# The copy of the turned queries or keys ahead of the exponential, in the last step of each attention unit

## The chip, the cores and the metric

The kernel runs on one NeuronCore of one Trainium2 chip. The metric is the device time of one execution in microseconds (us). Five engines work side by side, each through its own queue in order: TensorE (PE; its weight loads are shown apart as PEld), ScalarE (ACT), VectorE (DVE), GpSimd (POOL) and SyncE (SP), which issues most transfers. They meet through semaphores.

## What is computed

The reference runs two transformer blocks one after the other on 1024 tokens of width 1024. The change lies in the attention of the second block:

```python
def _attend_dense(q, k, v):
    s = jnp.einsum('bqhd,bkhd->bhqk', q, k, preferred_element_type=jnp.float32) * (QK_DIM ** -0.5)
    pr = jax.nn.softmax(s, axis=-1).astype(v.dtype)
    return jnp.einsum('bhqk,bkhd->bqhd', pr, v)

def _attend_latent(q, k_lat, v_lat, k_ctx, v_ctx):
    k_all = jnp.concatenate([k_lat, k_ctx], axis=1)
    v_all = jnp.concatenate([v_lat, v_ctx], axis=1)
    ...
```

There are 8 heads with queries and keys of 96 numbers and values of 64, 1024 queries in 8 blocks of 128, and 1280 keys (1024 of the tokens, 256 of the context). Ahead of it come the first block (windowed attention and a squared-ReLU network) and the second block's projections and Fourier mixer; behind it the merge of the two branches, a router and 16 experts.

## The kernel before, in words

**Precision.** Every operand of a matrix product is held as two parts: ACT copies a value and rounds it (the high part, "hi"), DVE subtracts that copy from the value (the low part, "lo"), and a product is three matmuls, hi by hi, hi by lo and lo by hi (`mm3`, lines 98 to 100). So whatever TensorE turns or multiplies passes through ACT and then DVE before TensorE can use it again.

**Rows and units.** A row `m` is one head and one block of 128 queries: head `m // 8`, block `m % 8`, 64 rows in all. Its logits are 128 by 1280. They stand in PSUM in one of two places, chosen by `m % 2` (`s_of`, line 2304), so the logits of row m+2 can be written only when the exponential of row m has been read out. A unit `u` is two rows, and there are 32 of them, four to a head (below they are called the units g = 0, 1, 2 and 3 of a head, g being `u % 4`). A unit has five steps t = 0 to 4, and the running number of a step is n = 5u + t. `STEPS` (line 2358) starts two units early, at n = -10.

**A step.** All three engines walk the same list of steps, each with a program of its own (`attn_pe` line 2432, `attn_act` line 2517, `attn_dve` line 2595). In step t of unit u, in this order:

- TensorE turns four 128 by 128 blocks of the exponentials of rows 2u and 2u+1 (line 2471) into one of two PSUM banks; multiplies turned blocks of earlier steps by the values (line 2482: one group of four in t = 0, 1 and 4, two in t = 3, none in t = 2); writes a piece of the logits of row 2u+4 or 2u+5 (lines 98 to 100); and in some steps turns a piece of queries or keys of a later head (line 2442) into the next of the two banks.
- ACT makes the high part of the turned exponentials (line 2572, tile MP_hi); runs an exponential over 128 by 1280 (line 2538, tile PB), that of row 2u+3 in t = 0 and that of row 2u+4 in t = 4; makes, where there is one, the high part of the turned queries or keys (line 2530, tiles qT_hi and kT_hi).
- DVE makes the low part of the turned exponentials (line 2665); in t = 2 the maximum of row 2u+4 and of the first 256 columns of row 2u+5 (lines 2613 and 2618), in t = 4 that of the other 1024 columns (line 2618) and the smaller of the two negated ones (line 2624); then the low part of the turned queries or keys (lines 2606 and 2608).

**Where queries and keys are turned** (`extra`, line 2320): queries of head h+2 in the last step (t = 4) of units 2 and 3 of head h, keys of head h+1 in the last step of units 0 and 1, and the last 256 keys in t = 1 of unit 0. So every last step has one, for as long as there is a later head: u = -2 to 25, 28 steps. In units 2 of heads 2, 4 and 6 ACT also spreads the inverse sums out in t = 0 and 1 (line 2581, tile `wide`, behind the exponential) and TensorE turns them in t = 1 and 2 (line 2509).

**The waits around it.** ACT's copy of turned queries or keys waits for TensorE's turning of them (line 2521). TensorE's logits wait in t = 0 for the exponential of row 2u+2, which is that of the last step of the unit before, and in t = 2 for that of row 2u+3 (line 2489). The two banks for turned blocks alternate: a turning waits until DVE has finished with the turning before the last (`t_free`, line 2413). Thus the turning in t = 1 waits for the low part of the queries or keys, and that in t = 2 for the low part of the turned exponentials of t = 0, or, where t = 1 turned something besides, for that of t = 1. The first logits of a new head, in t = 0 of unit 2, wait for the low part of the keys turned one step before (line 2492).

**The order is written twice.** `at_s` is a plan: a loop over the steps (lines 2365 to 2406) lists what each engine will finish, in order, and gives each entry its semaphore value; the programs assert that they come in that order. The change is therefore made in the plan and in `attn_act`.

Of the kernel before, what the change touches and what calls it, by code (L numbers as in the profile page):

```python
# [102 lines left out]
def _program(nc, A, out, ctx):  # L103
# [2194 lines left out]
    at_s = Stage(sem, "attn", pool=False)  # L2298
# [5 lines left out]
    def s_of(m, c0=0, c1=TA):  # L2304
        return S[:, TA * (m % 2) + c0:TA * (m % 2) + c1]

    def s_chunk(n):

        u, t = divmod(n, 5)
        m = 2 * u + 4  # L2310
        if not 0 <= m < 2 * N_U:
            return []
        return [[(m, 0, 512)], [(m, 512, 1024)], [(m, 1024, 1280), (m + 1, 0, 256)], [(m + 1, 256, 768)],
                [(m + 1, 768, 1280)]][t]

    def times_v_in(n):

        return [x for x in {0: (n - 2,), 1: (n - 2,), 2: (), 3: (n - 3, n - 2), 4: (n - 2,)}[n % 5] if 0 <= x < 5 * N_U]

    def extra(n):  # L2320


        u, t = divmod(n, 5)
        h, g = divmod(u, 4)
        x = {(2, 4): ("turn_q", h + 2, 0), (3, 4): ("turn_q", h + 2, 1), (0, 1): ("turn_k", h + 1, 2),
             (0, 4): ("turn_k", h + 1, 0), (1, 4): ("turn_k", h + 1, 1)}.get((g, t))
        if x and x[1] < 8:
            return x
        if 0 < t < 3 and (g == 2 and h in (2, 4, 6) or u == N_U - 1):
            return "row", 3 if u == N_U - 1 else h // 2 - 1, t - 1  # L2330
        return None

    def exp_at(n):

        u, t = divmod(n, 5)
        m = {0: 2 * u + 3, 4: 2 * u + 4}.get(t, -1)
        return m if 0 <= m < 2 * N_U else None

    def pair_of(n):

        u, t = divmod(n, 5)
        h, g = divmod(u, 4)
        return 3 if u >= N_U - 2 else h // 2 - 1 if h in (2, 4, 6) else None

    def is_invert(n):
        u, t = divmod(n, 5)
        return t == 4 and (u % 4 == 1 and u // 4 in (2, 4, 6) or u == N_U - 2)

    def is_wide(n):
        u, t = divmod(n, 5)  # L2350
        return t < 2 and (u % 4 == 2 and u // 4 in (2, 4, 6) or u == N_U - 1)

    def split_at(n):

        u, t = divmod(n, 5)
        return u - 28 if t == 4 and 28 <= u < 31 else None
# [8 lines left out]
    for n in STEPS:  # L2365
        u, t = divmod(n, 5)
        x = extra(n)
        if t == 2 and 0 < u <= N_U:
            at_s.act.plan(("low", u - 1))
            at_s.dve.plan(("out", u - 1))  # L2370
        if 0 <= n < 5 * N_U:
            at_s.pe.plan(("turn", n))
            at_s.act.plan(("turn", n))
            at_s.dve.plan(("turn", n))
            t_last.append(("turn", n))
        at_s.pe.plan(*[("times_v", x) for x in times_v_in(n)])
        if s_chunk(n) and t in (2, 4):
            at_s.pe.plan(("logits", 2 * u + 4 + t // 4))
            at_s.dve.plan(*(("max", 2 * u + 4), ("part", 2 * u + 5, 0)) if t == 2 else
                          (("part", 2 * u + 5, 1), ("max", 2 * u + 5)))  # L2380
        if exp_at(n) is not None:
            at_s.act.plan(("exp", exp_at(n)))
        if is_wide(n):
            at_s.act.plan(("wide", pair_of(n), t))
        if x:
            at_s.pe.plan(x)
            if x[0] != "row":
                at_s.act.plan(x)
                at_s.dve.plan(x)
            elif x[1] < 3:  # L2390
                at_s.dve.plan(x)
            if x[0:2] != ("row", 3):
                t_last.append(x)
        if is_invert(n):
            at_s.dve.plan(("inverse", pair_of(n)))
        if split_at(n) is not None:
            at_s.act.plan(("split", split_at(n)))
        if split_at(n - 2) is not None:
            at_s.dve.plan(("split", split_at(n - 2)))
        if n == 5 * N_U - 1:  # L2400
            at_s.dve.plan(("row", 3, 0))
            at_s.act.plan(("split", 3, 0))
        if n == 5 * N_U + 3:
            at_s.dve.plan(("split", 3, 0), ("row", 3, 1))
            at_s.act.plan(("split", 3, 1))
            at_s.dve.plan(("split", 3, 1))
# [3 lines left out]
    def t_bank(*x):  # L2410
        return B_MT[t_seq[x] % 2]
# [10 lines left out]
    def o_col(c):  # L2422
        return Q[:, :, 192 * c:192 * c + 128]

    def heads_of(who):
        return (Q, 8, qT) if who == "turn_q" else (K_, 10, kT2)
# [90 lines left out]
    def attn_act(act):  # L2517
        def turn_heads(who, h, i):
            D, nb, dst = heads_of(who)
            w = min(512, nb * P - 512 * i)  # L2520
            act.wait_ge(*at_s.pe(who, h, i))
            if h > 1:
                act.wait_ge(*at_s.pe("logits", 8 * (h - 2) + 7))
            elif (who, h) == ("turn_k", 1):
                act.wait_ge(*hd.pe("v", 9))
            scale = 1.0
            if who == "turn_q":
                act.wait_ge(*hd.dve("gqk"))
                scale = GQK[0:96, :]
            act.e.activation(dst[h % 2][0][0:96, 512 * i:512 * i + w], psum[0:96, t_bank(who, h, i), 0:w],  # L2530
                             ACT.Copy, scale=scale).then_inc(*at_s.act.one(who, h, i))

        def exponential(m):
            c, z = m // 16, 2 * (m % 8) + m // 8 % 2
            act.wait_ge(*(at_s.dve("max", m) if m % 2 else at_s.dve("part", m + 1, 0)))
            if m > 4:
                act.wait_ge(*at_s.pe("turn", 5 * ((m - 5) // 2) + 4))
            act.e.activation(PB[m % 5][:], s_of(m), ACT.Exp, bias=nmx[:, m % 8:m % 8 + 1],  # L2538
                             accum_out=msum(c)[:, z:z + 1]).then_inc(*at_s.act.one("exp", m))

        def split(c, i, *mark):
            sl = slice(4 * i, 4 * i + 4) if mark else slice(0, 8)
            act.wait_ge(*at_s.dve("row", c, i))
            act.wait_ge(*at_s.pe("turn_k", 7, 1))
            act.e.activation(o_of(c, 0)[:, sl, :], o_col(c)[:, sl, :], ACT.Copy).then_inc(
                *at_s.act.one("split", c, *mark))

        for i in range(2):
            turn_heads("turn_q", 0, i)
        for n in range(2):  # L2550
            v_act(act, n)
        for i in range(3):
            turn_heads("turn_k", 0, i)
        for n in STEPS:
            u, t = divmod(n, 5)
            for b in v_at(n):
                v_act(act, b)
            if t == 2 and 0 < u <= N_U:
                v = u - 1
                h = v // 4  # L2560
                r0, s0 = 64 * (h % 2), 64 * (1 - h % 2)
                act.wait_ge(*at_s.pe("times_v", 5 * v + 4))
                if v > 1:
                    act.wait_ge(*at_s.dve("out", v - 2))
                act.e.activation(o_low[v % 2][r0:r0 + 64, :],
                                 bank(B_MO, 0, 256)[s0:s0 + 64, :],
                                 ACT.Copy).then_inc(*at_s.act.one("low", v))
            if 0 <= n < 5 * N_U:
                act.wait_ge(*at_s.pe("turn", n))
                if n > 3:  # L2570
                    act.wait_ge(*at_s.pe("times_v", n - 4))
                act.e.activation(MP[n % 4][0][:], bank(t_bank("turn", n)), ACT.Copy).then_inc(  # L2572
                    *at_s.act.one("turn", n))
            if exp_at(n) is not None:
                exponential(exp_at(n))
            if is_wide(n):
                c = pair_of(n)
                act.wait_ge(*at_s.dve("inverse", c))
                if c:
                    act.wait_ge(*at_s.pe("row", c - 1, t))  # L2580
                act.e.activation(wide[t][:].rearrange("p n (h d) -> p (n h) d", h=2),
                                 rinv[:, 8 * t:8 * t + 8].unsqueeze(2).to_broadcast([P, 8, 64]),
                                 ACT.Copy).then_inc(*at_s.act.one("wide", c, t))
            x = extra(n)
            if x and x[0] != "row":
                turn_heads(*x)
            if n in ao_made:
                make_hi(act, T_AO[ao_made[n]])
            if split_at(n) is not None:
                split(split_at(n), 1)  # L2590
            if n == 5 * N_U - 1:
                split(3, 0, 0)
        split(3, 1, 1)
# [926 lines left out]
```

## Time and profile before

| | |
|---|---|
| median of 3 runs | 2296.77 us (2295.7 to 2297.83) |
| span of the profiled execution | 2296.6 us |
| TensorE busy over the span | 97% |
| VectorE busy over the span | 63% |
| ScalarE busy over the span | 42% |
| the attention of the second block | about 1460 to 1795 us |

The profile is of one execution; its span is taken as that execution's own time, since the page gives no other. A line of the timeline gives the start of an instruction in us from the start of the span, its length, its engine, line of the kernel and operation, and the tile that it writes and reads. A square bracket at its end gives the time for which the engine stood idle before it and what ended that wait. Neighbouring equal instructions are merged, with their number behind an x. The ends of matmuls are modelled, their starts are not.

### The profile page before, as it was taken

How to read it: one execution, taken by the hardware profiler on the slowest of the kernel's cores; microseconds unless marked ns; L12 is line 12 of the kernel's file. 1: busy time of each engine (PE TensorE's matmuls, PEld its weight loads, DVE VectorE, ACT ScalarE, POOL GpSimd, SP SyncE). 2: the span in 40 equal slices, each digit the busy share in tenths (PEclk: the TensorE clock that was granted, in tenths of full speed). 3: DMA queues.
4: the chain of work that ended last, by engine and by line, in shares of the span. 5: the costliest groups of instructions: out<-in, count | busy, mean ns of one | idle time of the engine just before them, and what ended most of it. 6: DMA issues, size and time to landing. Idle time of an engine off the chain costs nothing.

```text
span 2296.6 us, 27818 instructions
## 1 busy us (share of the span) xinstructions
PE 2222.8 (97%) x11316; PEld 1856.7 (81%) x11316; DVE 1450.6 (63%) x2316; ACT 971.2 (42%) x1521; POOL 214.8 (9%) x316
## 2 busy tenths in 40 slices
PE   8999999999999999999999999999998999899997
PEld 6898788888888888887888898788887886688886
DVE  7777445465564555567623227378887754799996
ACT  6777422111111111134422224366766322478785
POOL 0011000011010010100000014000000100211211
PEclk9999999999999999999999999999999999899998
DMA  3123512242342343323122112000001612799996
GB/s 146 47 79 122 195 46 61 81 138 87 98 137 92 101 133 97 110 102 67 54 79 92 35 45 88 28 1 1 1 1 42 256 55 102 299 393 386 386 379 225
DMA packets 79872, 280.64 MB, mean 122 GB/s; under 512 B 9936, under 2 KB 10224, under 8 KB 78592
## 3 DMA queue, kind: packets, MB, share of 16 engines
q1 hardware_dynamic: 48960, 172.84, 21.1%
q0 software_dynamic: 29632, 101.83, 14.2%
q10 hardware_dynamic: 1152, 4.19, 0.5%
q8 instruction: 89, 1.46, 0.3%
q14 instruction: 39, 0.32, 0.0%
HBM read 243.17 MB, written 35.66 MB: 121 GB/s over the span
## 4 chain that ended last, share of the span: by engine, by line
PE 86%; DVE 7%; ACT 4%; issue 1%; DMA 1%; POOLq 0%; SPq 0%; ACTq 0%; DVEq 0%
PE psum L98 26%; PE psum L100 25%; PE psum L99 25%; PE psum L2471 2%; PE psum L2482 2%; ACT MP_hi L2572 1%; PE psum L978 1%; DVE MP_lo L2665 1%; ACT PB L2538 1%; DVE small L2618 1%; PE psum L951 1%; PE psum L3309 1%; PE psum L3038 1%; DVE idx L3011 1%; DVE cur L3014 0%
## 5 line engine op out<-in xcount | busy, mean ns | idle before, releaser
L98 PE MATMUL psum<-U_hi,w_hi 128*128 128x512 f32 x688 | 271.0, 394 | 13.4 <-DVE w_lo L243 10.7
L234 ACT ACTIVATE w_hi<-raw 128x1024 fp32r<-128x1024 f32 (+2 forms) x163 | 162.7, 1002 | 280.5 <-PE psum L100 267.7
L99 PE MATMUL psum<-U_lo,w_hi 128*128 128x512 f32 x688 | 269.0, 391 | 0.0
L100 PE MATMUL psum<-U_hi,w_lo 128*128 128x512 f32 x688 | 268.7, 391 | 0.0
L243 DVE TENSOR_TENSOR w_lo<-raw,w_hi 128x1024 fp32r<-128x1024 f32 (+2 forms) x162 | 187.9, 1167 | 113.3 <-ACT w_hi L234 113.1
L98 PE MATMUL psum<-W_hi,w_hi 128*128 128x512 f32 x512 | 199.7, 390 | 0.9 <-DVE X L1092 0.9
L100 PE MATMUL psum<-W_hi,w_lo 128*128 128x512 f32 x512 | 199.2, 389 | 0.0
L99 PE MATMUL psum<-W_lo,w_hi 128*128 128x512 f32 x512 | 199.2, 389 | 0.0
L98 PE MATMUL psum<-a_hi,w_hi 128*128 128x512 f32 x512 | 199.2, 389 | 0.0
L99 PE MATMUL psum<-a_lo,w_hi 128*128 128x512 f32 x512 | 199.2, 389 | 0.0
L100 PE MATMUL psum<-a_hi,w_lo 128*128 128x512 f32 x512 | 199.2, 389 | 0.0
L98 PEld LDWEIGHTS psum<-U_hi,w_hi 128*128 128x128 f32 x688 | 129.8, 189 | 41.3 <-DVE w_lo L243 11.0
L1222 ACT ACTIVATE a_hi<-relu 128x512 fp32r<-128x512 f32 x64 | 40.2, 631 | 285.2 <-DVE relu L1247 285.2
L1276 DVE TENSOR_TENSOR X<-psum,X 128x512 f32<-128x512 f32 x128 | 85.4, 689 | 117.8 <-PE psum L100 117.8
L100 PEld LDWEIGHTS psum<-U_hi,w_lo 128*128 128x128 f32 x688 | 129.6, 188 | 27.4
L99 PEld LDWEIGHTS psum<-U_lo,w_hi 128*128 128x128 f32 x688 | 129.8, 189 | 25.2 <-issue 0.2
L1199 DVE CUSTOM_DVE_ANT_0 mraw<-mraw,srow 128x512 f32<-128x512 f32 x128 | 84.8, 689 | 101.2 <-DMA mraw<-in_w_mod 95.9
L2665 DVE TENSOR_TENSOR MP_lo<-psum,MP_hi 128x512 fp32r<-128x512 f32 x160 | 109.6, 686 | 55.8 <-ACT MP_hi L2572 55.0
L243 DVE TENSOR_TENSOR w_lo<-rawe,w_hi 128x1024 fp32r<-128x1024 f32 x112 | 131.4, 1220 | 10.2 <-ACT w_hi L234 9.7
L2572 ACT ACTIVATE MP_hi<-psum 128x512 fp32r<-128x512 f32 x160 | 95.5, 597 | 85.5 <-PE psum L2471 84.9
L1185 POOL DMA_DIRECT2D mraw<-in_w_mod x128 | 68.8, 538 | 659.3 <-DVE modb L1199 375.6
L234 ACT ACTIVATE w_hi<-rawe 128x1024 fp32r<-128x1024 f32 x112 | 116.3, 1058 | 23.9 <-PE psum L100 23.9
(441 smaller groups left out, 5185.8 us busy)
## 6 DMA issues: line engine op xcount, KB each, us to landing
rawe<-in_w_e SPq DMA_DIRECT2D x112, 512.0 KB, 16.9
mraw<-in_w_mod POOLq DMA_DIRECT2D x128, 256.0 KB, 3.0
rawx<-in_w_e SPq DMA_DIRECT2D x56, 512.0 KB, 18.0
raw<-in_w_up SPq DMA_DIRECT2D x32, 512.0 KB, 3.6
raw<-in_w_dn SPq DMA_DIRECT2D x32, 512.0 KB, 3.6
raw<-in_w_e SPq DMA_DIRECT2D x24, 512.0 KB, 17.0
X<-in_xT SPq DMA_DIRECT2D x8, 512.0 KB, 9.4
raw<-in_w_q SPq DMA_DIRECT2D x8, 512.0 KB, 4.9
```

The lines of the kernel that those rows point to most:

```text
L98: e.matmul(o, l[0], r[0], start=first, stop=False, skip_group_check=skip)
L99: e.matmul(o, l[0], r[1], start=False, stop=False, skip_group_check=skip)
L100: return e.matmul(o, l[1], r[0], start=False, stop=last, skip_group_check=skip)
L234: act.e.activation(hi, src, ACT.Copy).then_inc(w_hi, 1)
L243: dve.e.tensor_tensor(lo, src, f(hi), ALU.subtract).then_inc(w_lo, 1)
L1185: pool.e.dma_start(mraw[n % 2][:], A["w_mod"][mod_jobs[n][1]]).then_inc(mraw_in[n % 2].sem, 16)
L1199: dve.e.tensor_tensor_reduce(mraw[n % 2][:], mraw[n % 2][:], srow[:, half(i % 2)], 1.0, 0.0, ALU.mult, ALU.add, dst).then_inc(*ml.dve.one( ...
L1276: dve.e.tensor_tensor(X[:, n, half(h)], bank(dn_b[i, n, h]), X[:, n, half(h)], ALU.add).then_inc(*ml.dve.one("x", i, n, h))
L2471: m = pe.e.transpose(bank(t_bank("turn", n), 256 * kb + P * i, 256 * kb + P * i + P), PB[(2 * u + i) % 5][:, (2 * t + kb) * P:(2 * t + kb ...
L2482: m = pe.e.matmul(bank(B_MO, 0, 256), VV[:, 2 * y + kb, v // 4, :], MP[n0 % 4][x][:, 256 * kb:256 * kb + 256], start=(y, kb, x) == (0, 0, ...
L2572: act.e.activation(MP[n % 4][0][:], bank(t_bank("turn", n)), ACT.Copy).then_inc(*at_s.act.one("turn", n))
L2665: dve.e.tensor_tensor(lo[:], bank(t_bank("turn", n)), f(hi[:]), ALU.subtract).then_inc(*at_s.dve.one("turn", n))
```

## The change

In steps with t = 4, and in no others, ACT makes the high part of the turned queries or keys first and runs the exponential behind it. Where the last step turns neither, and in t = 0, the order stays. No instruction is added or taken away, and no other engine's program is touched.

```diff
@@ -2378,7 +2378,7 @@
             at_s.pe.plan(("logits", 2 * u + 4 + t // 4))
             at_s.dve.plan(*(("max", 2 * u + 4), ("part", 2 * u + 5, 0)) if t == 2 else
                           (("part", 2 * u + 5, 1), ("max", 2 * u + 5)))
-        if exp_at(n) is not None:
+        if exp_at(n) is not None and t < 4:
             at_s.act.plan(("exp", exp_at(n)))
         if is_wide(n):
             at_s.act.plan(("wide", pair_of(n), t))
@@ -2391,6 +2391,8 @@
                 at_s.dve.plan(x)
             if x[0:2] != ("row", 3):
                 t_last.append(x)
+        if exp_at(n) is not None and t == 4:
+            at_s.act.plan(("exp", exp_at(n)))
         if is_invert(n):
             at_s.dve.plan(("inverse", pair_of(n)))
         if split_at(n) is not None:
@@ -2571,7 +2573,7 @@
                     act.wait_ge(*at_s.pe("times_v", n - 4))
                 act.e.activation(MP[n % 4][0][:], bank(t_bank("turn", n)), ACT.Copy).then_inc(
                     *at_s.act.one("turn", n))
-            if exp_at(n) is not None:
+            if exp_at(n) is not None and t < 4:
                 exponential(exp_at(n))
             if is_wide(n):
                 c = pair_of(n)
@@ -2584,6 +2586,8 @@
             x = extra(n)
             if x and x[0] != "row":
                 turn_heads(*x)
+            if exp_at(n) is not None and t == 4:
+                exponential(exp_at(n))
             if n in ao_made:
                 make_hi(act, T_AO[ao_made[n]])
             if split_at(n) is not None:
```

## Rows read from the trace of the kernel before

**Rows 1.** The page's first line.

```profile
span 2296.6 us, 27818 instructions
```

**Rows 2.** The attention stage: length, busy PE, PEld, DVE, ACT, POOL; granted clock; DMA.

```profile
1475.00:1795.00 320.00, 301.37 (x2060) 260.34 (x2059) 251.77 (x389) 217.57 (x379) 2.12 (x4) 0.99 0.03 10
```

**Rows 3.** Waits within 1475 to 1795 us: waiter, releaser, us in total, times, longest.

```profile
PE psum L98 <- DVE kT_lo L2608: 6.2, 7, 0.9
...
PEld psum L98 <- ACT PB L2538: 0.6, 1, 0.6
```

**Rows 4.** Timeline, last step of a unit g = 0 (keys) and what follows.

```profile
1536.99 1.32 ACT L2538 ACTIVATE PB<-psum,small 128x1280 f32<-128x1280 f32 x1
...
1537.47 0.60 PE L2442 MATMUL psum<-ident,K 128*96 128x128 f32 x4
...
1538.29 0.59 ACT L2530 ACTIVATE kT_hi<-psum 96x512 fp32r<-96x512 f32 x1
...
1538.77 0.59 ACT L2572 ACTIVATE MP_hi<-psum 128x512 fp32r<-128x512 f32 x1
1538.84 0.40 PE L98 MATMUL psum<-kT_hi,qT_hi 96*128 96x512 f32 x1
...
1539.80 0.66 PE L2471 MATMUL psum<-ident,PB 128*128 128x128 f32 x4
```

**Rows 5.** Timeline, the same place behind a unit g = 1 (keys, new head next).

```profile
1546.34 0.60 PE L2442 MATMUL psum<-ident,K 128*96 128x128 f32 x4
...
1547.92 0.68 DVE L2608 TENSOR_TENSOR kT_lo<-psum,kT_hi 96x512 fp32r<-96x512 f32 x1
...
1548.75 0.47 PE L98 MATMUL psum<-kT_hi,qT_hi 96*128 96x512 f32 x1 [0.88 <-DVE kT_lo L2608]
...
1549.51 0.60 PE L2471 MATMUL psum<-ident,PB 128*128 128x128 f32 x4
```

**Rows 6.** Timeline behind a unit g = 1 of head 2, with the spreading of the inverses.

```profile
1586.31 0.64 ACT L2581 ACTIVATE wide<-small 128x512 f32<-128x512 f32 x1
...
1587.05 0.60 ACT L2572 ACTIVATE MP_hi<-psum 128x512 fp32r<-128x512 f32 x1
...
1588.46 0.62 PE L2471 MATMUL psum<-ident,PB 128*128 128x128 f32 x4
```

**Rows 7.** Timeline, last step of a unit g = 2 (queries) and what follows.

```profile
1555.99 0.60 PE L2442 MATMUL psum<-ident,Q 128*96 128x128 f32 x4
...
1556.81 0.68 ACT L2530 ACTIVATE qT_hi<-psum,vec 96x512 fp32r<-96x512 f32 x1
...
1557.38 0.59 ACT L2572 ACTIVATE MP_hi<-psum 128x512 fp32r<-128x512 f32 x1
...
1558.37 0.66 PE L2471 MATMUL psum<-ident,PB 128*128 128x128 f32 x4 [0.15 <-DVE qT_lo L2606]
```

**Rows 8.** Timeline behind a unit g = 3: ACT's copy in t = 1, TensorE's turning in t = 2.

```profile
1568.09 0.60 ACT L2572 ACTIVATE MP_hi<-psum 128x512 fp32r<-128x512 f32 x1
...
1569.46 0.66 PE L2471 MATMUL psum<-ident,PB 128*128 128x128 f32 x4
```

**Rows 9.** Timeline, last step of the first early unit (u = -2): the first exponential.

```profile
1472.49 1.28 ACT L2538 ACT_TABLE_LOAD   x1
...
1475.27 0.60 PE L2442 MATMUL psum<-ident,Q 128*96 128x128 f32 x4
...
1475.93 1.33 ACT L2538 ACTIVATE PB<-psum,small 128x1280 f32<-128x1280 f32 x1 [2.16 <-DVE small L2618]
...
1477.40 0.19 PEld L98 LDWEIGHTS psum<-kT_hi,qT_hi 96*128 96x128 f32 x1 [0.57 <-ACT PB L2538]
```

**Rows 10.** Stretches of time: length, busy PE, PEld, DVE, ACT, POOL; granted clock; DMA.

```profile
1464.00:1468.00 4.00, 1.89 (x12) 1.17 (x10) 1.63 (x5) 1.51 (x3) 0.00 (x0) 1.00 0.00 0
1468.00:1472.00 4.00, 3.46 (x10) 2.77 (x11) 1.51 (x3) 0.85 (x3) 0.00 (x0) 0.58 0.00 0
1772.00:1776.00 4.00, 2.40 (x20) 1.96 (x18) 2.14 (x5) 4.00 (x8) 1.05 (x2) 1.00 0.60 196
```

## The prediction

> **What bounds the kernel now.** The page comes first, for the span [rows 1], then the stretch in which the change lies: of the 320 us from 1475 to 1795 TensorE is busy for 301, DVE for 252, ACT for 218 [rows 2]. TensorE sets the pace, but with two thirds of ACT's and four fifths of DVE's time taken, both stand close behind. What is to be read is therefore who makes TensorE wait, and at which step. The waits of the stage [rows 3] say it: TensorE's logits waited once for an exponential (0.6 us), and 7 times for the low part of the turned keys, 0.9 us each. In every other unit the exponential of the last step is done before TensorE asks for it.
>
> How nearly so is read from the timeline of one unit [rows 4]. ACT starts the exponential at 1536.99, half a microsecond before TensorE turns the keys (1537.47), and copies them behind it, at 1538.29. TensorE starts the logits that overwrite the exponential's source at 1538.84. The price of the exponential for TensorE is read at its one wait [rows 9]: from its start (1475.93) to the first weight load that waited for it (1477.40) it is 1.47 us, since the reading of the accumulator comes behind it. In rows 4 it is thus free at 1538.46, 0.38 us early. That is all the slack there is.
>
> **The change, part by part.** Nothing is added: 28 copies, in the last steps of u = -2 to 25, go ahead of 28 exponentials. What changes is what each waits for. The exponential waits for nothing new by itself, but ACT takes its instructions in order, so behind the copy it inherits the copy's wait: TensorE has to finish turning the keys, the last thing it does in the step. ACT, which has time before that turning and none after it, idles before and pays after. Queued behind it on ACT are the copy and the exponential of t = 0 and the copy of t = 1; waiting for those are DVE's low parts, and TensorE.
>
> *Durations.* On ACT, start to next start: exponential 1.30 (1536.99 to 1538.29), copy of keys 0.48 (1538.29 to 1538.77) [rows 4], copy of queries 0.57 (1556.81 to 1557.38) [rows 7]. Logits that start after a wait take 0.76 to the next turning (1548.75 to 1549.51) [rows 5]. For the end of a turning I take its start plus 0.60. What a semaphore takes to release ACT no row here shows: nothing is the one end; the other is the 0.15 by which TensorE started (1548.75) after the low part's end (1547.92 + 0.68) [rows 5]. I take nothing, and leave 0.15 times the 27 boundaries that cost, 4.0 us, for the range.
>
> *Behind units g = 0 (7 of them, heads 0 to 6)* [rows 4]. Turning ends 1537.47 + 0.60 = 1538.07; copy there, 0.22 earlier than now; exponential at 1538.55; TensorE free of it at 1538.55 + 1.47 = 1540.02, where it now starts at 1538.84: a wait of 1.18. Next turning at 1540.02 + 0.76 = 1540.78 against 1539.80. Today's turning at 1539.80 has itself waited, for DVE's low part of the keys, and shows 0.66 instead of the 0.60 of one that has not [rows 4, 5]; that 0.06 and the wait are absorbed. Net 0.92 each, **6.4 us**. Nothing later in the unit gives it back, as the waits of the stage name none of TensorE there that could shrink [rows 3].
>
> *Behind g = 1, plain (heads 0, 1, 3, 5; 4 of them)* [rows 5]. Copy 1546.94, exponential 1547.42, free 1548.89; TensorE starts today at 1548.75, held back by the low part of the keys. That low part does not move: DVE starts it at 1547.92, without an idle bracket, behind its maximum. So the cover is the old wait and only 0.14 sticks out: **0.6 us**.
>
> *Behind g = 1, with the spreading (heads 2, 4, 6)* [rows 6]. TensorE's logits are again 0.14 late, but ACT is late by more. Its copy in t = 0 moves as in g = 0, to 1538.55 + 1.30 = 1539.85 against 1538.77: 1.08. Here the spreading moves from 1586.31 to 1587.39; the copy of t = 1 goes to 1587.39 + 0.64 = 1588.03; from such a copy to the turning in t = 2, with DVE's low part between, it is 1.37 (1568.09 to 1569.46) [rows 8], which gives 1589.40 against 1588.46: 0.94 each, **2.8 us**.
>
> *Behind g = 2 (heads 0 to 5)* [rows 7]. Turning ends 1556.59; copy; exponential 1557.16; free 1558.63; next turning 1559.39 against 1558.37, less 0.06: 0.96 each, **5.8 us**.
>
> *Behind g = 3 (heads 0 to 5)* [rows 8]. Here ACT already sets the pace: the copy of t = 1 at 1568.09 has no idle bracket, and the turning of t = 2 waits for its low part, because t = 1 turns keys as well. So ACT's own delay passes through whole: copy of t = 0 at 1557.16 + 1.30 = 1558.46 against 1557.38 [rows 7], 1.08 each, **6.5 us**.
>
> *The two early units.* In u = -2 the first exponential has its table load ahead of it, at 1472.49, hidden today because ACT then waits 2.16 us more for DVE [rows 9]. Changed, the copy starts at 1475.27 + 0.60 = 1475.87 and ends its turn at 1476.44. If the load stays ahead of the copy, TensorE is free at 1477.91, 0.5 late; if it goes with the exponential behind the copy, 1.28 are added, and it is 1.8 late. I take **1.8**, since the load stands at the exponential's line. The Trainium skill (ScalarE: Activation LUTs, Step-by-step: what each stage is for) has the compiler place the load right before the activation that needs it, at about 2.7 us with its drain; by that figure the last term would be 3.2 and the sum 25.3. The load's row agrees with neither part beyond its own 1.28 us: no row here shows a drain. In u = -1 logits come only after two projections of values, which cover the exponential: nothing.
>
> Sum: 6.4 + 0.6 + 2.8 + 5.8 + 6.5 + 1.8 = 23.9 us. No transfer and no queue of POOL or SP is passed. The stages behind take the delay whole. The base is the profiled execution, 2296.6 [rows 1], within 0.2 of the median shown, 2296.77: 2320.5 us.
>
> **The rivals.**
>
> *It isn't slower.* The place is the low part of the keys, for which TensorE waits 7 times behind g = 1. Were DVE waiting for ACT's copy there, the earlier copy (1546.94, where three units elsewhere have it behind an exponential) would cut the wait: at most 6.2 us in all [rows 3], 2290.4. It decides from the point where DVE is free before the copy ends, and only if the delay of the exponential is covered too. Against it: DVE starts that low part without a gap behind its maximum [rows 5], and behind g = 0 the exponential is early by 0.38 us and moves by 1.56 [rows 4]. Chance 0.03.
>
> *Nothing to be measured.* TensorE could reach the logits later than I read, so that the exponential stays covered, or ACT could catch up within t = 0. For it: the waits are short. Against it: the logits' starts are not modelled. 2297. Chance 0.03.
>
> *Half.* The delay is partly made good in the unit, where today small waits stand that I count only once. About 12 us, 2309. Chance 0.07.
>
> *The clock.* From 1464 to 1468 TensorE was busy for 1.89 of 4 us, and then the granted clock was 0.58 of full over 4 us, the lower of the two levels (1.2 of 2.4 GHz) for most of it [rows 10]; that lost 4 times 0.42, 1.7 us. If each of the 22 new waits of about a microsecond brought that, it would be 37 us more, 2358. Against it: 2.40 busy of 4 left the clock at 1.00 [rows 10], and a microsecond's wait leaves some 2.8. Chance 0.04; once, in u = -2, where TensorE would idle for over 2 us, it may come, and 1.7 is in the range. TensorE: Matmul & The Clock Gate (What's actually happening) in the Trainium skill has the clock held down by default and released by activity, so that idling gives it back; rows 10 agree for the fall, and by that rule alone any new wait counts for this rival.
>
> **How the numbers follow.** Forecast 0.83, half 0.07, clock 0.04, nothing 0.03, not slower 0.03. Likeliest: 2320.5. Upwards the semaphores (4.0), the clock once (1.7), and the drain and the stages behind, whose own clock may fall differently (2 to 3): 2329. Downwards the load ahead of the copy (1.3), starts read wrongly by 0.1 in 27 places (2.7), the stages behind (3), and a part of "half": 2312. Between the two lie 8 in 10. About 0.2% (4.6 us) is what a measurement of this kernel can tell from no change; so faster 0.02, same 0.04, slower 0.94.
>
> **What would show it.** In the waits of the stage a new line, TensorE's logits waiting for the exponential of line 2538, some 20 times at 1.1 to 1.3 us; ACT's copies of queries and keys waiting for TensorE's turning in all last steps; TensorE's busy time unchanged, the stage 22 to 26 us longer; behind g = 3 and the spreading, the wait in t = 2 for DVE's low part longer; the wait for the low part of the keys gone as a releaser, though not as time; the table load behind 1475.9. I am wrong if logits in t = 0 start within 0.5 us of the weighted values before them, or if the clock falls inside the stage.

## The result, and the profile after

The changed kernel takes 2322.59 us (median of 4 runs, 2321.83 to 2323.7) against 2296.36 for the kernel before in the same comparison: the ratio is 1.0113, with a 95% interval of 1.0101 to 1.0125. It is 26.2 us slower. The forecast was 2320.5 with a range of 2312 to 2329. The profiled execution has a span of 2320.8, 24.2 over that of [rows 1].

Lines in the changed kernel stand two further down in `attn_act` (the exponential is L2540, the copy of queries or keys L2532, that of turned exponentials L2574) and in `attn_pe` (L2444 turns queries and keys, L2473 exponentials), four in `attn_dve` (L2612, L2610, L2669 are the low parts of keys, queries and turned exponentials).

From the page of the changed kernel, its first line, the engines' busy time, and the head of the chain that ended last:

```profile
span 2320.8 us, 27818 instructions
PE 2224.6 (96%) x11316; PEld 1860.5 (80%) x11316; DVE 1452.5 (63%) x2316; ACT 973.2 (42%) x1521; POOL 214.6 (9%) x316
...
PE 88%; ACT 5%; DVE 5%; DMA 1%; issue 1%; POOLq 0%; SPq 0%; ACTq 0%; DVEq 0%
```

As many instructions as before; no engine's busy time has grown by more than 2 us, that of the weight loads by 4. The 24 us are idle time. Where, the stretch of the attention says, which answers to [rows 2] (columns as there):

```profile
1475.00:1819.00 344.00, 301.29 (x2044) 261.49 (x2043) 251.71 (x386) 219.12 (x377) 2.12 (x4) 0.99 0.03 9
```

TensorE is busy for 301 us, as before, in a stretch 24 us longer. And the waits from 1475 to 1820 us, against [rows 3], say for what:

```profile
PEld psum L98 <- ACT PB L2540: 36.5, 27, 2.5
PE psum L98 <- ACT PB L2540: 30.8, 27, 2.1
ACT kT_hi L2532 <- PE psum L2444: 18.3, 21, 1.0
ACT qT_hi L2532 <- PE psum L2444: 13.9, 13, 1.6
...
PE psum L2473 <- DVE MP_lo L2669: 6.4, 16, 1.1
```

Before, the logits waited once for an exponential. Now they do 27 times, 30.8 us in all: in every last step but that of u = -1. The 7 waits for the low part of the keys are gone, as a releaser. And ScalarE's copies now wait for TensorE's turning in all last steps.

The timeline of one such place, behind a unit g = 0, answers to [rows 4] line by line:

```profile
1542.45 0.60 PE L2444 MATMUL psum<-ident,K 128*96 128x128 f32 x4
...
1543.09 0.59 ACT L2532 ACTIVATE kT_hi<-psum 96x512 fp32r<-96x512 f32 x1 [1.02 <-PE psum L2444]
...
1543.58 1.31 ACT L2540 ACTIVATE PB<-psum,small 128x1280 f32<-128x1280 f32 x1
...
1544.88 0.59 ACT L2574 ACTIVATE MP_hi<-psum 128x512 fp32r<-128x512 f32 x1
1545.04 0.50 PE L98 MATMUL psum<-kT_hi,qT_hi 96*128 96x512 f32 x1 [1.07 <-ACT PB L2540]
...
1545.84 0.60 PE L2473 MATMUL psum<-ident,PB 128*128 128x128 f32 x4
```

The story is all in the brackets. ScalarE stands idle for 1.02 us until the keys are turned, copies them, and only then starts the exponential; TensorE stands idle for 1.07 us until that is read out. From the start of the turning to the next turning of exponentials it was 2.33 us (1537.47 to 1539.80); now it is 3.39 (1542.45 to 1545.84).

Behind g = 3 and where the inverses are spread, the wait in t = 2 for the low part of t = 1 has become longer too (0.50 here, in head 2, where [rows 6] shows none; about 0.2 behind g = 3, where [rows 8] shows none):

```profile
1597.35 0.59 ACT L2574 ACTIVATE MP_hi<-psum 128x512 fp32r<-128x512 f32 x1
...
1598.72 0.66 PE L2473 MATMUL psum<-ident,PB 128*128 128x128 f32 x4 [0.50 <-DVE MP_lo L2669]
```

The first exponential, against [rows 9]:

```profile
1473.61 0.60 PE L2444 MATMUL psum<-ident,Q 128*96 128x128 f32 x4
...
1474.25 0.69 ACT L2532 ACTIVATE qT_hi<-psum,vec 96x512 fp32r<-96x512 f32 x1 [3.24 <-PE psum L2444]
...
1474.95 1.28 ACT L2540 ACT_TABLE_LOAD   x1
...
1476.25 1.33 ACT L2540 ACTIVATE PB<-psum,small 128x1280 f32<-128x1280 f32 x1
...
1477.72 0.50 PE L98 MATMUL psum<-kT_hi,qT_hi 96*128 96x512 f32 x1 [2.12 <-ACT PB L2540]
```

The table load stands behind the copy, 1.28 us long, and the exponential follows 0.02 us after it. From turning the queries to the logits it was 2.13 us (1475.27 to 1477.40) and is 4.11 (1473.61 to 1477.72): 1.98 more.

What each place costs can be read off both traces by the start of ScalarE's copy in t = 4 of each unit: how much further apart two neighbouring ones stand than in the kernel before. Mean over the places of a kind, in us:

```
behind                      places   forecast   measured   sum
g = 0                          7       0.92       1.01      7.1
g = 1, heads 0, 1, 3, 5        4       0.14       0.21      0.8
g = 1, heads 2, 4, 6           3       0.94       0.91      2.7
g = 2                          6       0.96       1.04      6.2
g = 3                          6       1.08       1.13      6.8
u = -2                         1       1.8        1.98      2.0
u = -1                         1       0          0         0
sum                                   23.9                 25.6
```

### The profile page after: what moved, and what is told of

The parts are those of the page before. It is cut to its first block, busy times and chain, and to the rows that moved or that the text cites. A ratio compares the mean times of both kernels' runs of the same rounds, so it can differ in the third digit from the quotient of the medians.

```text
span 2320.8 us, 27818 instructions
## 1 busy us (share of the span) xinstructions
PE 2224.6 (96%) x11316; PEld 1860.5 (80%) x11316; DVE 1452.5 (63%) x2316; ACT 973.2 (42%) x1521; POOL 214.6 (9%) x316
## 4 chain that ended last, share of the span: by engine, by line
PE 88%; ACT 5%; DVE 5%; DMA 1%; issue 1%; POOLq 0%; SPq 0%; ACTq 0%; DVEq 0%
PE psum L98 26%; PE psum L99 26%; PE psum L100 26%; PE psum L2484 2%; ACT PB L2540 2%; PE psum L2473 2%; PE psum L978 1%; PE psum L951 1%; ACT MP_hi L2574 1%; PE psum L3313 1%; PE psum L3042 1%; PE psum L2444 1%; DVE idx L3015 1%; DVE MP_lo L2669 1%; DVE cur L3018 0%
## 5 line engine op out<-in xcount | busy, mean ns | idle before, releaser
L2669 DVE TENSOR_TENSOR MP_lo<-psum,MP_hi 128x512 fp32r<-128x512 f32 x160 | 110.1, 689 | 78.8 <-ACT MP_hi L2574 78.6
L2574 ACT ACTIVATE MP_hi<-psum 128x512 fp32r<-128x512 f32 x160 | 95.2, 595 | 81.2 <-PE psum L2473 80.7
```

What stands on the lines that cost most here:

```text
L2669: dve.e.tensor_tensor(lo[:], bank(t_bank("turn", n)), f(hi[:]), ALU.subtract).then_inc(*at_s.dve.one("turn", n))
```

## The experiments

Each time is the median of 4 to 11 executions, taken beside 15 or 25 of the kernel before on the same chip; "over" means over its median in that comparison (2296.6 to 2297.3).

### The change in parts

The condition `t == 4` in plan and program was narrowed, and `t < 4` became its opposite:

```diff
-            if exp_at(n) is not None and t == 4:
+            if exp_at(n) is not None and exp_last(n):
...
+    def exp_last(n):
+        u, t = divmod(n, 5)
+        return t == 4 and u >= 0 and u % 4 == 0
```

with `u % 4 == 1`, `u % 4 > 1` and, in the last one, `u < 0` in place of both.

> The order is changed in the last steps of the units g = 0 alone (7 places, heads 0 to 6). Theory (behind the copy the exponential inherits its wait for TensorE's turning, and TensorE's next logits wait for the exponential): about 1.0 us per place, 7.1 us over the kernel before, and the waits show TensorE's logits waiting for the exponential 7 times at 1.0 to 1.1 us more than today's one. Rival (each of the 28 swapped places costs the same, since it is the swap on ScalarE that costs): 26.2 / 28 = 0.94 each, 6.6 us; this run alone can't tell the two apart, it fixes the price of this kind of place. Rival (the clock): 12 us, with a granted clock below 1.00 inside the stage.

Measured 2303.46, 6.9 over; ratio 1.0029 (1.0019 to 1.0039). Per place 0.99 to 1.03 in the trace, nothing at the other places.

> The order is changed in the last steps of the units g = 1 alone (7 places, heads 0 to 6), where TensorE already waits 0.88 us for the low part of the keys. Theory: in heads 0, 1, 3 and 5 the old wait covers the new one but for 0.2 us; in heads 2, 4 and 6 ScalarE also spreads the inverses and is late by its own delay, 0.9 us; 4 times 0.2 and 3 times 0.9 are 3.6 us over the kernel before, and the wait for the low part of the keys is replaced by one for the exponential. Rival (the same price everywhere): 7 times 0.94, 6.6 us. Rival (an earlier copy helps TensorE, which waits for the keys here): 0 to 6 us faster than before.

Measured 2300.06, 3.5 over; 1.0015 (1.0006 to 1.0024). In the trace the four plain places cost 0.19 to 0.22 and the three with the spreading 0.91 to 0.92.

> The order is changed in the last steps of the units g = 2 and g = 3 from u = 0 on (12 places, heads 0 to 5). Theory: 6 times 1.03 and 6 times 1.13, 13.0 us over the kernel before; behind g = 3 the wait of the turning in t = 2 for the low part remains, 0.2 us, and behind g = 2 the 0.15 us wait for the low part of the queries is gone. Rival (the same price everywhere): 12 times 0.94, 11.2 us.

Measured 2310.19, 13.6 over; 1.0054 (1.0040 to 1.0068). Places: 1.02 to 1.06 behind g = 2, 1.13 to 1.14 behind g = 3.

> The order is changed in the two early units alone (u = -2 and -1, 2 places). Theory: 2.0 us from the first exponential, with its table load behind the copy, and up to 1.3 more where TensorE's idle time of 2.1 us brings the clock down; u = -1 costs nothing. 2.0 to 3.3 us over the kernel before. Rival (the same price everywhere): 1.9 us, half of it in u = -1.

Measured 2299.32, 2.7 over; 1.0014 (1.0005 to 1.0023). One wait of 2.1 us for the exponential, none in u = -1.

The four add to 26.6 us against 26.2 for the change as a whole, each known to within 2 to 4 us, and in the traces every kind of place has the same price alone as in the whole change, within 0.02 us: the places do not help or hinder each other. The even price of 0.94 is out: behind g = 1 it would have been 6.6, outside the interval, and the trace shows two prices there. An earlier copy of the keys does not help TensorE either.

### Is it the order, or the wait?

```diff
             if exp_at(n) is not None:
+                x = extra(n)
+                if t == 4 and x:
+                    act.wait_ge(*at_s.pe(*x))
                 exponential(exp_at(n))
```

> The order of the kernel before, exponential first and copy behind it, but in the last steps the exponential also waits for TensorE's turning of the queries or keys. So the order is the old one and only the wait is new. Theory (what costs is the wait that the exponential takes over, not the order): 24 to 28 us over the kernel before, as much as the change or a little more, since now the low part of the queries and keys is late as well: behind every g = 1 about 1.0 instead of 0.2 and 0.9 us; the first exponential costs nothing, since its table load stays ahead. Rival (the order costs: a copy in front holds up what is queued behind it on ScalarE by its own length, 28 times 0.5): no more than 3 us over the kernel before.

Measured 2330.86, 34.0 over; 1.0149 (1.0134 to 1.0165). The timeline behind a unit g = 0 (the copy of keys is L2530 here, DVE's low part of them L2611):

```profile
1546.45 0.60 PE L2442 MATMUL psum<-ident,K 128*96 128x128 f32 x4
...
1547.09 1.33 ACT L2538 ACTIVATE PB<-psum,small 128x1280 f32<-128x1280 f32 x1 [1.02 <-PE psum L2442]
...
1548.56 0.50 PE L98 MATMUL psum<-kT_hi,qT_hi 96*128 96x512 f32 x1 [0.58 <-ACT PB L2538]
...
1549.76 0.66 PE L2471 MATMUL psum<-ident,PB 128*128 128x128 f32 x4 [0.24 <-DVE kT_lo L2611]
```

With the old order and the new wait alone, ScalarE idles for the same 1.02 us, and the places cost as much as in the change or more: 0.99 us behind g = 0, 1.08 behind g = 2, 1.13 behind g = 3. So the wait costs.

The size was missed by 6 us, for two reasons that the trace shows. The table load did not stay ahead of the wait: it stands at 1476.56, behind it, and the early units cost 2.6 us where nothing was expected. And the clock fell inside the loop. Behind every g = 1 TensorE now waits 1.87 to 1.88 us for the low part of the keys. In heads 1, 2, 4 and 6 such a place costs 0.99 to 1.00 us, as expected; in heads 0, 3 and 5 it costs 2.54 to 2.57, and there the granted clock is at half (1.2 of 2.4 GHz) for 3.4 us right behind the wait. The 4 us around the wait and the 3.4 us that follow, first in head 0, then in head 1:

```profile
1513.40:1517.40 4.00, 2.13 (x16) 1.75 (x15) 3.06 (x5) 3.14 (x5) 0.00 (x0) 1.00 0.00 0
1517.40:1520.80 3.40, 3.40 (x14) 2.92 (x13) 1.03 (x3) 1.53 (x4) 0.00 (x0) 0.50 0.00 0
1556.08:1560.08 4.00, 2.12 (x16) 1.75 (x15) 3.06 (x5) 3.14 (x5) 0.00 (x0) 1.00 0.00 0
1560.08:1563.48 3.40, 3.40 (x27) 3.09 (x26) 1.32 (x4) 2.12 (x5) 0.00 (x0) 1.00 0.00 0
```

The three falls are 4.7 us of this execution. The places without them (27.2), the early units (2.6) and the falls add to 34.5, and its span is 34.4 over [rows 1]. Why the same wait brought a fall in three heads and not in four, no run here shows. Given the wait, the copy in front is the better order, by 34.0 - 26.2 = 7.8 us; the four plain units g = 1 are 3.1 of it (0.99 against 0.21 each), and most of the rest are the falls that the longer wait behind g = 1 brought.

### A delay without a wait

```diff
             if exp_at(n) is not None:
+                if t == 4 and extra(n):
+                    for i in (120, 121, 122, 45, 46, 47)[:2]:
+                        act.e.activation(vec[:, i:i + 1], EPSV, ACT.Copy)
                 exponential(exp_at(n))
```

> The kernel before with 2 copies of 128 by 1 ahead of the exponential in the 28 last steps: the exponential and the copy of the turned queries or keys behind it come later by d, which I estimate at 0.2 to 0.4 us; nothing waits for anything new. Theory, from the trace of the kernel before: the logits have 0.38 us of slack, the low part of the keys 0.15, that of the queries 0.07, ScalarE behind g = 3 none. So behind g = 0 and 1 it costs d - 0.15, behind g = 2 d - 0.07, behind g = 3 d: for d = 0.3, 14 times 0.15, 6 times 0.23 and 6 times 0.3 are 5.3 us over the kernel before. Rival (0.38 us is the slack everywhere, as the prediction said): nothing for d up to 0.38.

Measured 2299.27, 2.0 over; 1.0009 (1.0000 to 1.0018).

> The same with 6 such copies, d three times as long, 0.6 to 1.2 us. Theory: for d = 0.9, 14 times 0.75, 6 times 0.83 and 6 times 0.9 are 21 us over the kernel before, a little more where ScalarE spreads the inverses; a mere delay of the exponential by about a microsecond, with no wait for TensorE in it, costs about what the change costs. Rival (the change costs by TensorE and ScalarE waiting for each other, a delay alone would be caught up within the unit): under 10 us.

(with `[:6]` in the same edit.) Measured 2310.11, 12.9 over; 1.0058 (1.0044 to 1.0072). The lengths came out shorter than estimated, as the timeline shows, first of delay_two, then of delay_six:

```profile
1537.10 0.28 ACT L2577 ACTIVATE vec<-vec 128x1 f32<-128x1 f32 x2
1537.29 1.32 ACT L2538 ACTIVATE PB<-psum,small 128x1280 f32<-128x1280 f32 x1
```

```profile
1537.97 0.66 ACT L2577 ACTIVATE vec<-vec 128x1 f32<-128x1 f32 x6
1538.53 1.32 ACT L2538 ACTIVATE PB<-psum,small 128x1280 f32<-128x1280 f32 x1
```

So d is 0.19 and 0.56, not 0.3 and 0.9. With these the theory gives, behind g = 0 and 1, g = 2 and g = 3, 0.04, 0.12 and 0.19 for the one; the trace shows 0.02 to 0.05, 0.13 to 0.15, 0.17 to 0.19. For the other it gives 0.41, 0.49 and 0.56, and the trace shows 0.39 to 0.42, 0.50 to 0.52, 0.55 to 0.56. The sums, 2.4 and 12.0, lie within a microsecond of the measured 2.0 and 12.9. So 0.38 us is the slack of the logits alone. When exponential and copy move together, the copy's way through DVE gives out first, after 0.15 and 0.07 us, and behind g = 3 nothing is left at all. And a mere delay stays: it is not caught up within a unit.

### TensorE turns earlier

```diff
+            x = extra(n)
+            if x and t == 4:
+                turn_heads(*x)
             for m_, c0, c1 in s_chunk(n):
...
-            if x and x[0] != "row":
+            if x and x[0] != "row" and t < 4:
                 turn_heads(*x)
```

and the same in the plan, once on the changed kernel, once on the kernel before.

> The changed kernel, and besides TensorE turns the queries or keys ahead of the logits of the last step, not behind them. Theory: ScalarE's copy, and with it the exponential, comes earlier by as much as the turning does, about 0.5 us (it now waits for DVE's low part of two steps before), at 27 places; so some 11 to 13 us of the 26 are won back, and the waits of TensorE's logits for the exponential shrink from 1.1 to about 0.5 us. Rival (the wait for the turning plays no part): 26 us over the kernel before, as the change.

Measured 2315.76, 18.9 over; 1.0085 (1.0071 to 1.0098). The logits wait for the exponential 0.37 to 0.47 us, about as expected (behind g = 1 they wait 1.3 us for the low part of the keys instead), but only 7.3 us were won back, not 11 to 13. Hence its control:

> The control of turn_first: the order of the kernel before on ScalarE, with TensorE turning the queries or keys ahead of the logits of the last step. turn_first came out 18.9 us over the kernel before, where 13 to 15 were expected. Theory: the missing 4 to 6 us are the price of the earlier turning itself (it waits 0.1 to 0.2 us for DVE's low part of two steps before, and the logits of the last step and all that hangs on them come 0.4 us later), so this kernel is 4 to 7 us slower than the kernel before. Rival (the earlier turning is free, and the exponential behind the copy costs more than its wait): within 1 us of the kernel before.

Measured 2313.37, 16.4 over; 1.0073 (1.0059 to 1.0087). The earlier turning is far dearer than expected, in the old order as well. The waits of this control name the reason (L2613 and L2611 are DVE's low parts of keys and queries):

```profile
PE psum L98 <- DVE kT_lo L2613: 9.0, 7, 1.3
...
PE psum L2474 <- DVE qT_lo L2611: 6.6, 12, 0.6
...
PE psum L2474 <- DVE kT_lo L2613: 3.5, 7, 0.5
```

DVE takes the maximum of the logits of the last step before the low part of the keys or queries. With the turning in front those logits come about 0.6 us later, the low part with them, and the turning in t = 1 waits for it. So this pair says less than it was made for: the change costs 26.2 us with the late turning and 2.4 (18.9 less 16.4) with the early one, but that is partly because DVE's lateness now covers the exponential's. It agrees with the theory and can't prove it; the wait and the delay above do.

### The table load

```diff
+        act.e.activation(vec[:, 121:122], EPSV, ACT.Exp)
         for n in STEPS:
             u, t = divmod(n, 5)
             for b in v_at(n):
                 v_act(act, b)
```

> The changed kernel with one exponential of 128 by 1 ahead of the steps, so that the table load comes there and not behind the first copy of queries. The one number is written to a column that nothing reads. Theory: 1.3 us less than the change, and another 1.3 less where the fall of the clock behind TensorE's wait of 2.1 us is gone with it: 23.6 to 24.9 us over the kernel before; that first wait shrinks from 2.1 to 0.8 us. Rival (the load is hidden in the wait for the first maximum in either order): as the change, 26 us.

Measured 2320.41, 23.5 over; 1.0105 (1.0090 to 1.0121). The profile shows the load at 1468.98, ScalarE idle behind it, and the first wait down to 0.69 us, from 2.12:

```profile
1468.98 1.28 ACT L2556 ACT_TABLE_LOAD   x1
...
1475.96 0.51 PE L98 MATMUL psum<-kT_hi,qT_hi 96*128 96x512 f32 x1 [0.69 <-ACT PB L2540]
```

The load's part is 26.2 - 23.5 = 2.7 us by the medians. The two profiles show what it consists of. From the turning of the queries in u = -2 to ScalarE's copy in t = 4 of u = 0 it is 24.86 us here and 27.53 in the changed kernel, 2.7 less; 1.4 of it are the shorter wait, and the rest is a fall of the clock that the changed kernel's profile shows behind this wait and this one does not. In only_early the same wait of 2.1 us stands without a fall, and the stretch is 26.29: 1.2 less than in the changed kernel. So the fall costs 1.2 us where it comes, and it does not come in every execution.

### A better place for the keys

The waits of 0.9 us behind g = 1 stood in the kernel before already. Moving the second piece of the keys to t = 1 of the same unit is one line:

```diff
-               (0, 4): ("turn_k", h + 1, 0), (1, 4): ("turn_k", h + 1, 1)}.get((g, t))
+               (0, 4): ("turn_k", h + 1, 0), (1, 1): ("turn_k", h + 1, 1)}.get((g, t))
```

> The order of the kernel before; the second piece of the keys is turned, copied and made low in t = 1 of the units g = 1, not in t = 4 (7 pieces). Theory (TensorE's waits of 0.9 us behind g = 1 are for work put too late, not for lack of an engine): these 7 waits go, some of it comes back as a wait for the low part in t = 2, and in heads 2, 4 and 6 the spreading on ScalarE holds t = 1 as before; 2 to 6 us faster than the kernel before. Rival (VectorE or ScalarE is full there and the wait only moves): within 1 us of the kernel before.

Measured 2297.40 against 2296.90; 1.0001 (0.9992 to 1.0010). Behind the unit 1.40 us are won (0.30 with the spreading), within it 0.93 are lost: 0.43 for the turning itself, which has only moved, the rest a new wait in t = 2. It adds up to nothing.

> As keys_at_t1, but only in heads 0, 1, 3 and 5, where no inverses are spread behind the unit. The trace of keys_at_t1 gives 0.93 lost within such a unit and 1.40 won behind it, so 4 times 0.47, 1.9 us faster than the kernel before, at the edge of what can be measured. Rival (nothing is won anywhere): the same as the kernel before within 0.5 us.

Here the key of that entry was `(1, 4 if h in (2, 4, 6) else 1)`. Measured 2294.82, 2.1 under the kernel before; 0.9992 (0.9983 to 1.0001). The size is the expected one, but the interval still touches 1, so a gain is likely and not shown.

## Why the prediction was right

**What bounds the kernel.** Right. The attention is a loop in which TensorE has 0.38 us of slack against the exponential, and the change moves that by 1.6.

**Who pays for what.** Right in kind at every place of the loop, and only_g0, only_g1, only_g23 and only_early show it one kind at a time: about 1 us behind g = 0 and 2, almost nothing behind a plain g = 1, whose old wait is the cover, ScalarE's own delay behind g = 3 and the spreading, one table load, nothing in u = -1. That it is the inherited wait and not the order was argued in the prediction; wait_only shows it, with 0.99 behind g = 0 in the old order against 1.01 in the new.

**The sizes.** The sum was 1.7 us short of the 25.6 read from the traces, and small terms are missing in most places. A semaphore from TensorE to ScalarE takes 0.04 us (the turning ends at 1543.05, the copy starts at 1543.09), where I took nothing. Logits that have waited take 0.80 to the next turning (1545.04 to 1545.84), where [rows 5] gave 0.76. With both, 0.92 becomes 1.00, and 1.01 was measured behind g = 0. In u = -2 the load starts only when the copy has ended, 0.70 after the copy's start (1474.25 to 1474.95), where 0.57 was taken. The spreading came out 0.03 below its forecast, not above: ScalarE's copy follows it after 0.52 (1596.83 to 1597.35), not 0.64.

**The clock.** In u = -2 it came once in the profiled execution, as the range allowed. TensorE was busy for 1.88 of 4 us, and then:

```profile
1475.00:1479.00 4.00, 1.88 (x9) 1.23 (x8) 1.91 (x5) 3.99 (x5) 0.00 (x0) 1.00 0.02 4
1479.00:1482.00 3.00, 3.00 (x10) 2.37 (x9) 0.15 (x1) 0.66 (x3) 0.00 (x0) 0.56 0.00 0
```

the granted clock was 0.56 of full for 3 us, most of it at the lower of the two levels (1.2 of 2.4 GHz). Against only_early, which had the same wait and no fall, it cost 1.2 us. On the other hand the fall of [rows 10], from 1468 to 1472, did not take place in this execution, and the attention began 1.7 us earlier, 1.5 of it for that. So the span reads: 25.6 from the places, 1.2 from this fall, less 1.7 for the earlier start and about 1 behind the attention, is the 24.2 measured, within 0.1. None of the waits of 1.1 us brought the clock down, so the rival of the clock is out for the change. That it was not far off, wait_only shows: there, waits of 1.9 us in the same loop brought it down three times in seven.

**Its own signs.** The prediction called itself wrong if the clock fell inside the stage, and by that wording the fall in u = -2 is one, since the stage is counted from 1475. The sum's range had allowed for just this one, so the sign was worded too broadly. The logits wait for the exponential 27 times and not some 20, because behind each g = 1 the exponential takes the place of the keys as the last to come, and only what it comes later than they did is a cost.

**The rivals.** "Nothing", "half" and "not slower" fell by the result alone. Of "half" there is something after all, in the other direction: delay_two and delay_six show that small waits are indeed counted only once (0.15 and 0.07 us), and that nothing else is made good.

**A step that held by luck.** "That is all the slack there is" was too simple. 0.38 us is the slack of the logits; the copy behind the exponential has less, as the delays show. Since the change brings the copy forward, the smaller slack never came into play.

**The table load.** The forecast took 1.8 us for u = -2, with the load behind the copy; 1.98 came. The Trainium skill (ScalarE: Activation LUTs, Step-by-step: what each stage is for) has the load placed right before the activation that needs it; the trace agrees, at 1474.95. The 2.7 us with a drain that it gives there the trace does not bear out: the load is 1.28 long, ends at 1476.23, and the exponential starts at 1476.25.

## What to carry to other kernels

In an engine's queue that is worked off in order, an instruction also waits for everything that those before it wait for; here the exponential took over a wait of 1.02 us in this way. So before moving one ahead of another, compare when their inputs come, not how long they are. Where the inputs of one are there first and its reader has next to no slack, as with the exponential here, it goes first. That an engine is often idle says little (ScalarE was idle for a third of this stage): the price of a wait is read at its reader, place by place, since an old wait of the reader may cover it. Here the places of the loop had prices from 0.2 to 1.1 us.

## What the runs showed of the hardware

- A copy of 128 by 1 on ScalarE, from SBUF to SBUF, takes the queue for 0.09 us when several follow each other (6 of them moved the next instruction by 0.56).
- Nothing in the exponential's own length depends on what stands before it: 1.31 to 1.34 us in all orders.
- The same wait of TensorE brings its clock down at some times and not at others. After one of 2.1 us the granted clock fell in the changed kernel's profile and stayed at 1.00 in that of only_early, though TensorE had been busy for 1.88 of 4 us in both (1475.0 to 1479.0 and 1475.3 to 1479.3). Of seven waits of 1.9 us in wait_only three were followed by 3.4 us at half clock, each costing 1.6 us. Waits of 1.0 to 1.2 us once in about 10 us, 26 of them in the changed kernel, were followed by none.
- The table load takes 1.28 us and nothing behind it: the exponential starts 0.02 us after its end in the changed kernel, and 0.01 in wait_only (1476.56 + 1.28 to 1477.85).
